# Two modulation sums of a feed-forward half in one burst behind slab nineteen

## The reference, cut to what matters

```
def modulation(cond, w, b):
    m = jax.nn.silu(cond) @ w + b
    return m.reshape(cond.shape[0], 1, N_MOD, D_MODEL)     # N_MOD = 9
def modulate_in(x, g_pre, mod, j):
    return rmsnorm(x, g_pre) * (1.0 + mod[:, :, 3 * j + 1]) + mod[:, :, 3 * j]
def gated_residual(x, out, g_post, mod, j, weight):
    return x + weight * mod[:, :, 3 * j + 2] * rmsnorm(out, g_post)
def swiglu(h, w13, w2):
    a, g = jnp.split(h @ w13, 2, axis=-1)
    return (jax.nn.silu(g) * a) @ w2
```

## Time and profile before

| what | value |
|---|---|
| median of three runs | 2454.76 us (2453.8 to 2455.15) |
| the profiled execution | 2455.28 us |
| its span, first to last instruction | 2453.5 us |
| TensorE (PE) busy | 2406.3 us, 98% |
| weight loads of TensorE (PEld) | 2206.1 us, 90% |
| DVE busy | 1758.6 us, 72% |
| ACT busy | 981.8 us, 40% |
| POOL busy | 436.7 us, 18% |
| mean granted TensorE clock | 0.997 |

### The profile page before, as it was taken

The page is one execution under the profiler, slowest core; times in us unless marked ns, Lnnn a source line. Parts: engine busy times, 40 slices in busy tenths (PEclk is TensorE's granted clock), DMA queues, the critical chain, the costliest instruction groups (busy, mean ns, idle before and its releaser), DMA issues. The chain is left out here.

```text
span 2453.5 us, 38986 instructions
## 1 busy us (share of the span) xinstructions
PE 2406.3 (98%) x15173; PEld 2206.1 (90%) x15173; DVE 1758.6 (72%) x2469; ACT 981.8 (40%) x1917; POOL 436.7 (18%) x462
## 2 busy tenths in 40 slices
PE   6999999999999999999999999999999999999998
PEld 6998999889889789979988997998899879989997
DVE  4988786575554679878846878885587659856864
ACT  4442343533445455324435442443511154423432
POOL 1220121211115122103212210220300022201211
PEclk9999999999999999999999999999999999999999
DMA  7526334285212453343253426334154333243332
GB/s 228 164 61 211 100 87 142 95 261 160 54 51 74 108 181 87 131 153 89 76 172 115 132 72 213 89 87 163 30 186 148 108 115 88 72 147 99 87 128 96
DMA packets 347229, 297.96 MB, mean 121 GB/s; under 512 B 38799, under 2 KB 296839, under 8 KB 347047
## 3 DMA queue, kind: packets, MB, share of 16 engines
q1 hardware_dynamic: 341798, 278.64, 37.6%
q0 software_dynamic: 5248, 16.83, 1.8%
HBM read 280.57 MB, written 14.80 MB: 120 GB/s over the span
## 5 line engine op out<-in xcount | busy, mean ns | idle before, releaser
L2013 DVE TENSOR_TENSOR w_lo<-w_raw,w_hi 128x512 fp32r<-128x512 f32 (+1 forms) x249 | 211.4, 852 | 225.6 <-ACT w_hi L1419 224.3
L1419 ACT ACTIVATE w_hi<-w_raw 128x512 fp32r<-128x512 f32 (+1 forms) x249 | 188.0, 760 | 462.0 <-DMA w_raw<-in_ffn_w_dram 240.0
L913 PE MATMUL psum<-w_hi,act_hi 128*128 128x512 f32 x800 | 318.3, 398 | 0.0
L915 PE MATMUL psum<-w_hi,act_lo 128*128 128x512 f32 x800 | 317.2, 396 | 0.0
L914 PE MATMUL psum<-w_lo,act_hi 128*128 128x512 f32 x800 | 316.9, 396 | 0.0
L1046 PE MATMUL psum<-hT_hi,w_hi 128*128 128x320 f32 x912 | 281.9, 309 | 0.5 <-DVE z_quarters L2301 0.5
L1048 PE MATMUL psum<-hT_hi,w_lo 128*128 128x320 f32 x912 | 281.8, 309 | 0.0
L1047 PE MATMUL psum<-hT_lo,w_hi 128*128 128x320 f32 x912 | 281.8, 309 | 0.0
L1046 PE MATMUL psum<-t_hi,w_hi_more 128*128 128x320 f32 x608 | 187.9, 309 | 0.0
L1048 PE MATMUL psum<-t_hi,w_lo_more 128*128 128x320 f32 x608 | 187.9, 309 | 0.0
L1047 PE MATMUL psum<-t_lo,w_hi_more 128*128 128x320 f32 x608 | 187.8, 309 | 0.0
(11 more groups left out here) (303 smaller groups left out, 5929.8 us busy)
## 6 DMA issues: line engine op xcount, KB each, us to landing
w_raw<-in_ffn_w_dram SPq DMA_DIRECT2D x96, 512.0 KB, 5.0
w_raw_next<-in_ffn_w_dram SPq DMA_DIRECT2D x80, 512.0 KB, 5.2
w_raw<-in_ffn_w_dram SPq DMA_DIRECT2D x148, 256.0 KB, 3.4
ada_tile_ffn<-in_ada_w_dram SPq DMA_DIRECT2D x56, 512.0 KB, 4.1
ada_direct<-in_ada_w_dram POOLq DMA_DIRECT2D x32, 512.0 KB, 5.7
w_raw<-in_ab_w_in_dram SPq DMA_DIRECT2D x28, 512.0 KB, 4.1
w_raw<-in_sc_w_in_dram SPq DMA_DIRECT2D x24, 512.0 KB, 4.0
ada_tile_sc<-in_ada_w_dram SPq DMA_DIRECT2D x24, 512.0 KB, 4.0
```

The lines of the kernel that those rows point to most:

```text
L913: mm(out, a_hi, b_hi, start=first, stop=False)
L915: return mm(out, a_lo, b_hi, start=False, stop=final)
L1419: A(dst, src, ACT.Copy).then_inc(w_hi_ok, 1)
L2013: V.tensor_tensor(d_, a, b.bitcast(F32), ALU.subtract).then_inc(w_lo_ok, 1)
```

## The change

The first sum moves from behind unit 11 to behind unit 19, where the second one is, so that both are made one after the other; the second's rows go to columns 256 to 511 of the bank that holds the first's. Rows of both are made at unit 21 and stored together by `late_rows`. So that two sets can be alive at once there is a second tile for the rows (over `u_two`) and one for the bias (in the last quarter of `z_quarters`). The second bias is now loaded at unit 9 and not behind the first store. DVE waits for both sums before its rows; ACT's first `keep_one` of the second half waits until the rows are stored. FFN 5 has one sum only, which moves from unit 11 to unit 19. SP's wait for the first sum, quoted above, is unchanged.

```diff
-SUMS_AT = {"ffn": (11, 19), "ab": (6, 12), "sc": (11, 19, 99)}
-ROWS_AT = {"ffn": (13, 21), "ab": (7, 99), "sc": (13, 21, 99)}
-STORE_AT = {"ffn": (15, 99), "ab": (9, 15), "sc": (15, 23, 99)}
+SUMS_AT = {"ffn": (19, 19), "ab": (6, 12), "sc": (11, 19, 99)}
+ROWS_AT = {"ffn": (21, 21), "ab": (7, 99), "sc": (13, 21, 99)}
+STORE_AT = {"ffn": (99, 99), "ab": (9, 15), "sc": (15, 23, 99)}
...
+        ffn_rows = [mod_rows["ffn"], at("mod_rows_ffn2", [P, MW], tail + 8192 + 4096)]
+        ffn_bias = [mod_bias["ffn"], at("mod_bias_ffn2", [P, MW], where["silu_g"] + 4096)]
...
+        SUM_COL = lambda kind, z: slice(z * MW, (z + 1) * MW) if kind == "ffn" else slice(0, MW)
...
-                        load_bias_rows(ph["mb"], kind, *ph["mods"][0])
+                        load_bias_rows(ph, 0)
+                    if j == 8 and kind == "ffn":
+                        sp.wait_ge(act_ready, ph["ar"] + HF)
+                        load_bias_rows(ph, 1)
...
-                    if z:
+                    if z and kind != "ffn":
                         pe.wait_ge(mrow_ok, MROW(b - 1))
-                    elif kind == "ffn":
+                    elif z == 0 and kind == "ffn":
                         pe.wait_ge(q_summed, U_CROSS(ph["g1"] - 1))
...
-                            last = mm(PS[32 * i:32 * i + 2, SUM_BANK[kind][z], 0:MW], pick[:, 1 - cd:3 - cd], ...)
+                            last = mm(PS[32 * i:32 * i + 2, SUM_BANK[kind][z], SUM_COL(kind, z)], pick[:, 1 - cd:3 - cd], ...)
...
+                if ph["half"] and plan[s][0]["mods"]:
+                    act.wait_ge(mod_stored, STORED(plan[s][1]["mb"] - 1))
                 keep_one(ph, g0)
...
-            def modulation_rows(s, b, kind, bank):
+            def modulation_rows(s, b, kind, bank, z=0, n=1):
-                dve.wait_ge(mod_mm, MM(b))
-                dve.wait_ge(bias_in, BIAS(b))
-                need(dve, mod_stored, STORED(b - 1))
+                dve.wait_ge(mod_mm, MM(b - z + n - 1 if kind == "ffn" else b))
+                dve.wait_ge(bias_in, BIAS(b - z + n - 1 if kind == "ffn" else b))
+                need(dve, mod_stored, STORED(b - z - 1 if kind == "ffn" else b - 1))
```

More of the change, by code:

```diff
@@ L286, in build @@
         mod_bias = {kind: at(f"mod_bias_{kind}", [P, MW], top - MW * 4) for kind in STEPS}
+        ffn_rows = [mod_rows["ffn"], at("mod_rows_ffn2", [P, MW], tail + 8192 + 4096)]
+        ffn_bias = [mod_bias["ffn"], at("mod_bias_ffn2", [P, MW], where["silu_g"] + 4096)]
+        rows_of = lambda kind, z: ffn_rows[z] if kind == "ffn" else mod_rows[kind]
+        bias_of = lambda kind, z: ffn_bias[z] if kind == "ffn" else mod_bias[kind]
+        assert MW <= HT and 4096 + MW * 4 <= 2 * TOK * 4
         more_hi = at("w_hi_more", [P, 3, KH, P], where["gate"], F32R)
@@ L640, in load_gate, with load_bias_rows @@
                 dma(gpost[:], bass.AP(norm_g.tensor, norm_g[l, j, 1].offset, [[0, P], [1, D]])).then_inc(gate_loaded, 16)
-            def load_bias_rows(b, kind, layer, col):
-                need(sp, mrow_ok, MROW(b - 1))
+            def load_bias_rows(ph, z):
+                b, kind = ph["mb"] + z, ph["kind"]
+                layer, col = ph["mods"][z]
+                need(sp, mrow_ok, MROW(ph["mb"] - 1 if kind == "ffn" else b - 1))
                 for i in range(4):
                     src = bass.AP(ada_b.tensor, ada_b[layer, col + i * MW:].offset, [[0, 2], [1, MW]])
-                    dma(mod_bias[kind][32 * i:32 * i + 2, :], src).then_inc(bias_in, 16)
+                    dma(bias_of(kind, z)[32 * i:32 * i + 2, :], src).then_inc(bias_in, 16)
             def store_mod_rows(b, rows, layer, col):
@@ L676, in load_mods @@
                     if STORE_AT[kind][z] == u:
-                        store_mod_rows(ph["mb"] + z, mod_rows[kind], *ph["mods"][z])
+                        store_mod_rows(ph["mb"] + z, rows_of(kind, z), *ph["mods"][z])
                         if z + 1 < n:
-                            load_bias_rows(ph["mb"] + z + 1, kind, *ph["mods"][z + 1])
+                            load_bias_rows(ph, z + 1)
             def late_rows(ph):
@@ L1081, in modulation @@
                         for i in range(4):
-                            last = mm(PS[32 * i:32 * i + 2, SUM_BANK[kind][z], 0:MW], pick[:, 1 - cd:3 - cd], mod_acc[kind][z][cd][:, i * MW:(i + 1) * MW], start=(cd == 0), stop=(cd == 1))
+                            last = mm(PS[32 * i:32 * i + 2, SUM_BANK[kind][z], SUM_COL(kind, z)], pick[:, 1 - cd:3 - cd], mod_acc[kind][z][cd][:, i * MW:(i + 1) * MW], start=(cd == 0), stop=(cd == 1))
                     last.then_inc(mod_mm, 1)
@@ L2185, in modulation_rows @@
                     rows = slice(32 * i, 32 * i + 2)
-                    V.tensor_tensor(mod_rows[kind][rows, :], PS[rows, bank, 0:MW], mod_bias[kind][rows, :], ALU.add).then_inc(mrow_ok, 1)
+                    V.tensor_tensor(rows_of(kind, z)[rows, :], PS[rows, bank, SUM_COL(kind, z)], bias_of(kind, z)[rows, :], ALU.add).then_inc(mrow_ok, 1)
             def add_step(ph, j):
@@ L2204, in modulate_at @@
                     if ROWS_AT[ph["kind"]][z] == u:
-                        modulation_rows(ph["sub"], ph["mb"] + z, ph["kind"], SUM_BANK[ph["kind"]][z])
+                        modulation_rows(ph["sub"], ph["mb"] + z, ph["kind"], SUM_BANK[ph["kind"]][z], z if ph["kind"] == "ffn" else 0, len(ph["mods"]))
                 for j in range(8 * len(ph["mods"])):
```

## The result

The changed kernel takes 2464.42 us (median of six runs, 2463.35 to 2466.27); beside it the kernel before took 2455.31 us (six runs, 2453.8 to 2456.41). The ratio is 1.0037, with a 95% interval of 1.0028 to 1.0047: **9.1 us slower**, where +7.6 was forecast. The profiled execution took 2463.35 us, with a span of 2461.5 us and a mean granted clock of 0.998. Lines of the code lie 11 to 13 further down than before: the sum L1082 is L1093, the products' first line L1046 is L1057, L1560 is L1571, L2186 is L2199, L2250 is L2263, L2263 is L2276, `add_two` L2308, `add_five` L2314.

The account below looks back on a forecast made before the run. TensorE's work plus its waits was taken to bound the kernel. Late load +8.5 us, adjacent sums -0.9, hidden work 0: +7.6 us, from a median of 2454.76 to 2462.4 us, range 2456 to 2468.5.

Parts of the forecast that it names:

- What bounds the kernel: Whole kernel: TensorE, busy 98% of the span; a change gains only matmul time and loses where another engine stops PE.
- The burst, -0.29 per FFN: On TensorE: a second sum right behind the first costs 0.88 us, not 1.17; -0.9 us over three FFNs (-1.4 to 0).
- The load behind the sum, +8.5: Second half's first weights, loaded only after the first sum, make DVE late and PE wait: +8.5 us over four FFNs.
- the transfer: Second DMA of the first weight pair: lands 5.0 us after its issue in FFN 0, 5.6 in later ones.
- Where PE is stopped: Second half's first pairs: PE first misses DVE at product 6, waiting for `add_five`; in FFN 5 already at product 1.
- The sign that was announced: Among PE's waits, L1046 for L2301 once or twice per FFN, 1 to 3 us each, largest in FFN 5.
- What was hidden: Second bias load, row stores, second pair's load and `keep_one`'s new wait: all claimed to cost 0.
- The rival that the change is faster: Load hidden, only the saving from adjacent sums left: 0.9 us, at most 1.4; chance 0.03.
- The rival of the hidden transfer: Second DMA takes 3.8 us like a first, so the weight load is nearly hidden: +1, 2456 us; chance 0.22.
- The slower load: Second half's first weights land after 6.9 us in each FFN: 14 us lost, 2468 to 2469 us; chance 0.10.

Follow-up runs that it names:

- burst at 20: The changed kernel with the sums behind unit 20, one unit later than 19: 2482.45 us, ratio 1.0107.
- burst at 17 or 18: The changed kernel with the sums behind unit 17 (rows at unit 20): 2454.85 us; behind unit 18 (rows at 21): 2453.16 us, again on another chip 2455.42 us.

## Why the prediction was right, and by how much each step was off

**What bounds the kernel.** As forecast: the busy time of TensorE did not move, and the loss is a wait in the first pairs of the second halves. The burst at 20 shows that delay there is paid in full.

**The burst, -0.29 per FFN.** Measured 0.31 from starts. One group of 32 matmuls lasts 1.91 us, as said.

**The load behind the sum, +8.5.** The mechanism is shown from both sides: with the load early the loss is gone (first sum at 11, burst at 17 or 18), and with the late load alone in the old kernel it is there. The size was 11.4 by the starts (10.5 in the second trace of the same kernel). By steps of the sum:

| step | forecast | measured |
|---|---|---|
| SP issues after the sum begins | 1.15 | 1.16, 1.15, 1.16, 1.15 |
| the second tile lands after its issue | 5.0; 5.6 later on | 5.2, 5.8, 6.5, 6.2 |
| weight sums start after the sum begins | 6.65; 7.4 | 6.85, 7.69, 8.39, 8.02 |
| weight sums to the end of the second `add_five` | 24.7 | 24.87 |
| from there until PE starts | 0.06 | 0.14 |
| lost per FFN | 1.3, 2.1, 2.1, 3.0 | 1.75, 2.6, 3.3, 3.8 |

The term that was mis-sized is the transfer. The weight sums were later than forecast by 0.20, 0.29, 0.99 and 0.62 us, which is 2.1 of the 2.9 us that the sum missed. Within that, 0.13 us in each FFN is the time from the landing to DVE's start, which the sum had at nothing; the second issue in turn came 0.03 to 0.08 us sooner than forecast. In FFN 3 the landing is longest because SP's second issue is. SP in time order, FFN 3:

```profile
1540.06 2.28 SPq L600 DMA_DIRECT2D w_raw_next<-in_ffn_w_dram  x2
```

and the issue of the second, in a window of its own (KB, us to landing):

```profile
w_raw_next<-in_ffn_w_dram SPq DMA_DIRECT2D x1, 512.0 KB, 6.5
```

Two issues took 2.28 us where they take 1.01 in FFN 0. The 6.5 count from the second issue's start and so hold its 1.68 us. The mean of three rows had been used for it, 5.6; its upper rows, 5.9 and 6.9, were the better bound. The other 0.8 us or so are the two small steps of the table, some 0.2 us in each FFN. One of them was misread: in rows 11 `add_five` ends at 2077.47, and PE starts 0.14 us later, not 0.06, in the trace of before already:

```profile
2077.61 0.38 PE L1046 MATMUL psum<-hT_hi,w_hi 128*128 128x320 f32 x1 [0.52 <-DVE z_quarters L2301]
```

The net forecast of +7.6 lies nearer to the timed +9.1 than the steps do to the traces: there the change costs 10.9 and 10.0 us at the four places. That closeness is in part luck.

**Where PE is stopped.** The prediction said that the matmul that first misses DVE is product 6, with product 1 in FFN 5 alone. This was wrong in place, not in the sum. In FFN 0 PE stops first at product 4, which needs a low part, then at product 5 for `add_two`, then 0.17 us at product 6; in FFNs 2 and 3 already at product 1, as in FFN 5. DVE is one queue, so each of these is the same lateness met earlier, and the total is still set by `add_five` of the second pair: 31.72 (its end) + 0.14 = 31.86 in FFN 0. I had looked for the smallest slack only at `add_five`. For FFNs 2 and 3 the prediction's own numbers already gave a wait at product 1: DVE's first low part at 7.4 + 2.03 = 9.4 us, PE there at 8.1 + 0.88 = 9.0. That test was made for FFN 5 alone. The sign that was announced, waits for L2301 among PE's waits, did not appear for that reason.

**What was hidden.** Stores, bias loads and the wait of `keep_one` cost nothing that can be seen. ACT's copy in FFN 0, in time order:

```profile
268.95 0.42 ACT L1589 ACTIVATE u_two<-psum 128x320 f32<-128x320 f32 x1
```

It has no idle time for a store ahead of it, and it comes 4.5 us before DVE wants it (273.49). The kernels with the burst at 17 and 18 have the same eight stores and the same wait, and are not slower than before. The rival that the change is faster fell with the first result.

**The rival of the hidden transfer** (no change; the estimate from the Trainium skill's DMA page, some 4.4 us for the pair) is refuted: the pair landed 5.6 to 7.1 us after its first issue. The page (the Trainium skill, DMA: Bandwidth & Descriptors, Anatomy of one DMA) gives its fit for DMAs that GpSimd issues; these are issued by SP, so the fit was carried over to a case that it does not name. With nothing else on the queue at its issue, the follower took as long as in rows 9 or longer. **The slower load** was half true: 6.2 and 6.5 us in two FFNs, not the 6.9 in all.

**What stays open.** Why the same two DMAs land later in FFNs 2, 3 and 5 than in FFN 0, and why SP's second issue took so long in FFN 3, no run here tells. Neither is tied to this trace: over the eight profiled executions with a late load the second tile landed 5.2 to 5.7 us after its issue in FFN 0, 5.3 to 6.3 in FFN 2 and 6.0 to 6.5 in FFN 3, and the two issues took 1.8 to 2.5 us, where 1.26 is common, at one or two places in six of them, never in FFN 0.

## What to carry to other kernels

When a reader of a buffer is moved later, look for the transfer that is to overwrite the buffer: it waits for the reader, and the distance between reader and use must hold the whole transfer, issue and second landing included. How much lateness counts is read from the fixed order of the engine behind it, as the smallest distance from each of its results to the matmul that wants it, over more than one round. Here one unit of 3.5 us earlier turned +9 us into -2 (-0.6 by the traces), and one later cost 16 more; so such a place is tried at its neighbours before the idea is dropped.

## What the runs showed of the hardware that was not expected

- Two loads of 512 KB back to back, in the changed kernel: the first lands 3.8 to 4.6 us after its issue, the second 5.2 to 6.5 after its own, though nothing else was queued ahead of them.
- In the rows read here TensorE restarts 0.14 us after the DVE instruction that it waited for has ended, and the second matmul comes 0.07 to 0.10 us late. Waits up to 0.16 us leave no idle time in the record, since the records overlap.
- In waits of 3.7 to 5.0 us on TensorE (burst at 20) the granted clock fell to 0.50 and stayed there for some 6.8 us, four times in four. Shorter waits are not safe either: with waits of up to 1.8 us in the same place (burst at 19) it did not fall, with one of 1.86 us there (before with the late load, FFN 3) it did, for 3.4 us, and at the 2.23 us wait near 1930 us it fell in six of ten executions.
